# A two-layer S5/RWKV-7 decoder step on one core: transfers and first steps in another order, the token shift spread over scan steps, the feed-forward norm's root applied behind the products

## The chip, the cores and the metric

The kernel runs on one core of one Trainium2 chip. The core has TensorE for matmuls (they write PSUM banks), VectorE and ScalarE for elementwise work, POOL (GpSimd), and SP, which here only issues DMA transfers. In the profile they are PE, DVE, ACT, POOL and SP. The metric is the device time of one execution in microseconds; less is better.

## The reference

Each of two layers mixes tokens by two parallel branches out of one projection, and ends in a feed-forward part: dense in layer 0, a top-2-of-8 mixture in layer 1. There are 272 prompt positions and 8 sample tokens, T = 280 in all, and all data are float32.

```
def rmsnorm(x, g):
    y = xf * lax.rsqrt(jnp.mean(xf * xf, axis=-1, keepdims=True) + RMS_EPS)
    return (y * g.astype(jnp.float32)).astype(x.dtype)
def swiglu(h, w1, w3, w2):
    return (jax.nn.silu(h @ w1) * (h @ w3)) @ w2
# each layer
h = rmsnorm(x, W['norm_mix'][l]);  proj = h @ W['w_in'][l]
# branch A: S5 scan over proj[:, :512]; branch B: RWKV-7 over the next 1792 columns p
prev = jnp.concatenate([shift0[:, None], p[:, :-1]], axis=1)
z = p + (prev - p) * mu                     # the token shift
x = x + m @ W['w_out'][l]                   # m: the gated sum of both branches
h2 = rmsnorm(x, W['norm_ffn'][l])
x = x + swiglu(h2, W['ffn_w1'][j], W['ffn_w3'][j], W['ffn_w2'][j])    # layer 0
```

The root of the norm is one number per token. With g folded into x, h2 @ w1 equals the root times ((x*g) @ w1), so it can be applied to the product.

## The kernel before

Activations lie transposed: the 128 partitions are features, the 280 columns are tokens. A matrix of 1024 features is 8 tiles. All large weights come as slots of 1 MB through a ring of 7 slots in SBUF, issued by SP; a slot is refilled when `weights_used` says that it was read. Each engine has its own instruction list, written out by hand, and they meet only at semaphores. There is no scheduler: an instruction waits behind everything written ahead of it on its engine, and a DMA issue on ScalarE's or POOL's list stands in that list like any other instruction.

**Start.** SP issues the six transfers in `FIRST` and seven ring slots. ScalarE squares the tiles of x (`norm`, i = 0), then issues x0 and 14 constants, then takes the root. TensorE sums the squares with a matrix of ones (the ones products). VectorE takes the reciprocal and writes h in eight products, then runs `discretise` (small steps on 128x32), the products on x0, and `rotation_points`, whose sines ScalarE takes ahead of copying the projection's banks out. TensorE has three banks for projection tiles, so tile n waits for the copy of tile n - 3.

**Projection and scan.** 34 tiles of 8 products each. The first four are the S5 input u, the next 14 are RWKV rows (`prow`), 16 are gates. TensorE alternates: input products of two scan steps (`bu_pair`), four projection tiles, output products (`y5_pair`) of the pair before the last. VectorE runs `scan_pair` for j = 0, 2, ..., 14. POOL writes rotation tables (`rotations`) for each step into one of two buffers, and may do so when VectorE has read the table of two steps earlier. Behind pair 8 stands `shifted`, the whole token shift. Behind the scan come the low-rank products (`lora`), for which TensorE waits until VectorE has read the last input products and ScalarE has done its part on z.

**Feed-forward of layer 0.** Each weight slot is split into a high part (ScalarE, `fw_hi`) and a low part (VectorE, `fw_lo`), the activations likewise (`h_hi`, `h_lo`); a product is three matmuls, so a slot is 48. Before it stand the output projection (8 tiles, each added into x by VectorE), the squares, the ones products, root, reciprocal, eight products into h_f, both splits of h and the split of slot 0. In the loop ScalarE takes silu straight out of PSUM and VectorE multiplies it with the second bank. POOL loads layer 1's small weights (`s5_b`, `s5_c`, `lora_up`) as soon as layer 0's mixer is done.

## Time and profile before

| | us |
|---|---|
| median of 3 runs | 2256.25 |
| lowest, highest | 2254.21, 2258.53 |
| the profiled execution | 2257.98 |
| its span | 2255.8 |
| TensorE busy in it | 2056.7 |
| VectorE busy in it | 1573.3 |
| ScalarE busy in it | 1012.1 |
| POOL busy in it | 359.5 |

The span is the time from the first to the last instruction in one profiled execution. The busy share of an engine is an average over stages that are bound by different things. A timeline row tells when a run of equal instructions starts, how long it lasts, how many there are, and, in brackets, how long the engine idled before it and what released it. A matmul of 128x280 in float32 shows as two records, so a projection tile is x16 and four tiles are x64. PEclk is the TensorE clock that was granted, 1.00 being 2.4 GHz and 0.50 being 1.2 GHz. Layer 0's mixer takes 0 to 500, its feed-forward 500 to 722, layer 1's mixer follows, and the experts fill the rest from about 1,229 on.

### The profile page before, as it was taken

The page shows a single profiled execution, that of the slowest core. Times are in us where ns is not written, and L with a number is a line of the kernel's source. Part 1 is how long each engine was busy: PE and PEld are TensorE (multiplying, and loading weights), DVE is VectorE, ACT ScalarE, POOL GpSimd, SP SyncE. Part 2 cuts the span into 40 slices and gives each one's busy share as a digit, 9 for nine tenths or more (in the row PEclk, how much of TensorE's full clock was granted, in tenths as well). Part 3 has the DMA queues.
Part 4 walks back from the last instruction along what each step waited for, and adds up shares of the span by engine and source line. Part 5 has one row for each costly group of instructions (what it writes and reads, how often), then busy time and mean ns, then how long its engine had stood idle before and what let it go on. Part 6 is the DMA issues. An engine that isn't in the chain of part 4 may idle for free.

```text
span 2255.8 us, 29759 instructions
## 1 busy us (share of the span) xinstructions
PE 2056.7 (91%) x11490; PEld 1690.4 (75%) x11490; DVE 1573.3 (70%) x1960; ACT 1012.1 (45%) x1184; POOL 359.5 (16%) x315
## 2 busy tenths in 40 slices
PE   3998789898999997788895999999999999999996
PEld 2775577778999775577774888888888888888884
DVE  3586766325544777766324889898988889898984
ACT  1012323104433111333103777777767677777773
POOL 0553600200000554501201010101010100100000
PEclk7997999598999998999695999999999999999998
DMA  6333000144443333000142999999999999999990
GB/s 241 112 114 112 3 1 1 59 166 180 169 168 131 112 131 113 3 1 1 40 167 81 365 377 355 354 362 359 357 364 357 360 366 353 366 360 352 364 361 36
DMA packets 71627, 466.71 MB, mean 207 GB/s; under 512 B 12453, under 2 KB 13349, under 8 KB 16325
## 3 DMA queue, kind: packets, MB, share of 16 engines
q1 hardware_dynamic: 62352, 449.11, 53.7%
q0 software_dynamic: 3184, 13.24, 1.5%
q10 hardware_dynamic: 5956, 2.50, 0.4%
q8 instruction: 93, 1.52, 0.3%
q14 instruction: 42, 0.34, 0.0%
HBM read 459.74 MB, written 5.08 MB: 206 GB/s over the span
## 4 chain that ended last, share of the span: by engine, by line
PE 79%; DVE 7%; issue 6%; POOL 4%; ACT 2%; ACTq 1%; DMA 0%; SPq 0%; DVEq 0%; POOLq 0%
PE bank L526 77%; PE bank L1105 1%; ACTq L1183 1%; POOL arena L376 1%; DVE arena L1660 1%; PE bank L673 1%; ACT arena L1168 1%; POOL arena L390 1%; DVE arena L1490 0%; POOL arena L397 0%; DVE ring L1791 0%; DVE ring L1815 0%; DVE ring L1803 0%; ACT ring L1168 0%; POOL arena L408 0%
## 5 line engine op out<-in xcount | busy, mean ns | idle before, releaser
L2065 DVE TENSOR_TENSOR w_lo<-ring,w_hi 128x2048 fp32r<-128x2048 f32 x336 | 768.9, 2293 | 109.1 <-ACT w_hi L1168 108.7
L1168 ACT ACTIVATE w_hi<-ring 128x2048 fp32r<-128x2048 f32 x336 | 643.5, 1916 | 183.2 <-PE bank L526 183.2
L526 PE MATMUL bank<-arena,ring 128*128 128x280 f32 (+1 forms) x1920 | 460.6, 408 | 48.1 <-DVE arena L1490 23.0
L526 PEld LDWEIGHTS bank<-arena,ring 128*128 128x128 f32 (+1 forms) x1920 | 354.8, 190 | 143.4 <-issue 39.1
L1168 ACT ACTIVATE arena<-bank 128x256 f32<-128x256 f32 (+4 forms) x300 | 117.7, 396 | 592.2 <-PE bank L526 576.5
L526 PE MATMUL bank<-w_hi,he_hi 128*128 128x512 f32 x896 | 365.4, 408 | 4.9 <-DVE w_lo L2065 4.9
L526 PE MATMUL bank<-w_hi,he_lo 128*128 128x512 f32 x896 | 353.8, 395 | 0.0
L526 PE MATMUL bank<-w_lo,he_hi 128*128 128x512 f32 x896 | 353.4, 394 | 0.0
L526 PEld LDWEIGHTS bank<-w_hi,he_lo 128*128 128x128 f32 x896 | 169.0, 189 | 39.3
L526 PEld LDWEIGHTS bank<-w_hi,he_hi 128*128 128x128 f32 x896 | 169.1, 189 | 37.2 <-issue 5.3
L526 PEld LDWEIGHTS bank<-w_lo,he_hi 128*128 128x128 f32 x896 | 169.8, 190 | 32.4
L526 PE MATMUL bank<-ring 128*128 128x128 f32 (+6 forms) x1504 | 163.0, 269 | 31.9 <-DVE ring L1791 14.8
L526 PEld LDWEIGHTS bank<-ring 128*128 128x128 f32 (+3 forms) x1504 | 147.6, 171 | 49.7 <-DVE ring L1791 18.4
L526 PE MATMUL bank<-w_hi,at_hi 128*128 128x512 f32 x448 | 176.4, 394 | 0.0
L526 PE MATMUL bank<-w_hi,at_lo 128*128 128x512 f32 x448 | 176.4, 394 | 0.0
L526 PE MATMUL bank<-w_lo,at_hi 128*128 128x512 f32 x448 | 176.2, 393 | 0.0
L526 PE MATMUL bank<-arena 64*64 64x64 f32 (+12 forms) x1472 | 140.2, 307 | 34.8 <-DVE arena L1601 25.4
L526 PEld LDWEIGHTS bank<-arena 64*64 64x64 f32 (+6 forms) x1472 | 102.9, 179 | 76.5 <-issue 32.5
L1168 ACT ACTIVATE ring<-bank 128x256 f32<-128x256 f32 (+4 forms) x210 | 63.0, 358 | 169.2 <-PE bank L526 133.5
L496 POOL CAST rows<-arena 128x1 uint32<-128x1 f32 x8 | 13.9, 1732 | 763.9 <-ACT arena L1168 763.9
L1981 DVE TENSOR_TENSOR fw_lo<-ring,fw_hi 128x2048 fp32r<-128x2048 f32 x33 | 75.6, 2293 | 61.1 <-ACT fw_hi L1168 61.1
L526 PE MATMUL bank<-h_hi,fw_hi 128*128 128x280 f32 x352 | 103.6, 294 | 11.4 <-DVE fw_lo L1981 11.4
(261 smaller groups left out, 2634.9 us busy)
## 6 DMA issues: line engine op xcount, KB each, us to landing
ring<-wstream_dram SPq DMA_DIRECT2D x427, 1024.0 KB, 6.8
s<-s_dram POOLq DMA_DIRECT2D x2, 1024.0 KB, 14.7
o_rw_dram<-arena POOLq DMA_DIRECT2D x2, 1024.0 KB, 5.1
x<-x_dram SPq DMA_DIRECT2D x1, 1120.0 KB, 5.0
y_dram<-arena POOLq DMA_DIRECT2D x1, 1120.0 KB, 4.4
arena<-s_b_dram POOLq DMA_DIRECT2D x2, 512.0 KB, 7.5
arena<-s_c_dram POOLq DMA_DIRECT2D x2, 512.0 KB, 9.4
arena<-lora_up_dram POOLq DMA_DIRECT2D x2, 512.0 KB, 11.4
```

Source lines behind the costliest of these rows:

```text
L376: g.tensor_tensor(tc, ca, cb, ALU.mult)
L390: ins = g.tensor_scalar(chi[:, f, :], z[:, 4 + f, :], col(l, "k_k", f), None, ALU.mult)
L496: nc.gpsimd.tensor_copy(rows[:], slot_iw[:, e % 2, 0:1]).then_inc(S["rows_ready"], 1)
L526: return nc.tensor.matmul(out, lhsT, rhs, start=start, stop=stop, **k)
L673: last = nc.tensor.transpose(pools[4 * i][0:nt, j * P:(j + 1) * P], src, ident[:])
L1105: last = nc.tensor.transpose(pools[2][:, (t % 2) * FW + j * P:(t % 2) * FW + (j + 1) * P], act_e[:, t % 2, j * P:(j + 1) * P], ident[:])
L1168: return nc.scalar.activation(out, in_, func, **k)
L1183: ac.dma_start(t[:], a[n]).then_inc(S["consts"], 16)
L1660: ins = v.tensor_scalar(z[:, c, :], z[:, c, :], col(l, "mu", c), None, ALU.mult)
L1981: v.tensor_tensor(fw_lo[n % 2], slot(FFN_AT + n), fw_hi[n % 2].bitcast(F32), ALU.subtract)\
L2065: v.tensor_tensor(w_lo[n % SPLIT], slot(n), w_hi[n % SPLIT].bitcast(F32), ALU.subtract)\
```

## The change

1. **Transfers.** SP issues lam and tv first, under a semaphore of their own, then x, ones, eps and pv, ring slot 0, x0, the 14 constants, and only then ring slots 1 to 6. ScalarE issues none of them any more. POOL issues s0 behind the fourth table in place of before the first. Layer 1's small weights wait for the end of the feed-forward, since h_lo has moved to where they lie.
2. **First steps.** The discretisation up to the angles and layer 0's rotation points stand ahead of the first norm on VectorE, the rest behind it. `one_mu` holds 1 - mu.
3. **Token shift.** ScalarE writes (1 - mu) p into z as it copies a bank. VectorE adds mu times the previous column in one instruction for each tile, in groups of 4, 4, 4 and 2 behind the pairs 2, 4, 6 and 8.
4. **Feed-forward norm.** h_hi and h_lo are made from x times the gains, tile by tile, as the output projection adds into x. Slot 0 is split ahead of that. TensorE runs slot 0, then the ones products, in bank 4. VectorE multiplies both banks by the root's reciprocal as it takes them out of PSUM, into up_s and act_f; silu reads up_s.

```diff
--- before.py
+++ after.py
-        h_hi, h_lo = half("h_hi", 4480, DC, T), half("h_lo", 2048, DC, T)
+        h_hi, h_lo = half("h_hi", 4480, DC, T), half("h_lo", 8640, DC, T)
+        up_s = ar(7840, 2, T)
         act_hi, act_lo = half("act_hi", 10912, CF, T), half("act_lo", 17072, CF, T)
-        fw_hi = [half(f"fw_hi{i}", at, SLOT) for i, at in enumerate((0, 25280))]
-        fw_lo = [half(f"fw_lo{i}", at, SLOT) for i, at in enumerate((23232, 27328))]
+        fw_hi = [half(f"fw_hi{i}", at, SLOT) for i, at in enumerate((25280, 0))]
+        fw_lo = [half(f"fw_lo{i}", at, SLOT) for i, at in enumerate((27328, 23232))]
...
-        FIRST = [(x, "x"), (lam, "lam"), (ones, "ones"), (eps, "eps"), (pv, "pv"), (tv, "tv")]
+        FIRST = [(x, "x"), (ones, "ones"), (eps, "eps"), (pv, "pv")]
...
+            for t, n in ((lam, "lam"), (tv, "tv")):
+                sp.dma_start(t[:], a[n]).then_inc(S["lam_in"], 16)
             for t, n in FIRST:
                 sp.dma_start(t[:], a[n]).then_inc(S["first_in"], 16)
-
-            for s in range(RING):
+            sp.dma_start(ring[:, 0, :], a["wstream"][0]).then_inc(slot_in[0], 16)
+            sp.dma_start(x0[:], a["x0"]).then_inc(S["x0_in"], 16)
+            for t, n in CONSTS[1:]:
+                sp.dma_start(t[:], a[n]).then_inc(S["consts"], 16)
+            for s in range(1, RING):
...
-                    pool.wait_ge(S["x_ready"], 2 * l - 1)
+                    pool.wait_ge(S["x_ready"], 2 * l)
                 pool.wait_ge(S["first_in"], N_FIRST)
                 pool.dma_start(s5_b, a["s5_b"][l]).then_inc(S["small_w"], 16)
                 pool.dma_start(s5_c, a["s5_c"][l]).then_inc(S["small_w"], 16)
                 pool.dma_start(lora_up, a["lora_up"][l]).then_inc(S["small_w"], 16)
-                pool.dma_start(s0[:], a["s0"][l]).then_inc(S["s0_in"], 16)
-
                 for j in range(JT):
                     rotations(l, j)
+                    if j == 3:
+                        pool.dma_start(s0[:], a["s0"][l]).then_inc(S["s0_in"], 16)
...
-                norm(1 + 2 * l)
+                if l:
+                    norm(1 + 2 * l)
...
-                    pe.wait_ge(S["weights_used"], FFN_AT + n + 1)
+                    if n:
+                        pe.wait_ge(S["weights_used"], FFN_AT + n + 1)
                     if n >= 2:
                         pe.wait_ge(S["act_ready"], n - 1)
                     w_h, w_l = (t[n % 2].rearrange("p (c k m) -> p c k m", c=2, k=DC) for t in (fw_hi, fw_lo))
                     for c in range(2):
                         for k in range(DC):
-                            if n == 0 and c == 0 and k % 4 == 0:
-                                pe.wait_ge(S["h_split"], k // 4 + 1)
+                            if n == 0 and c == 0:
+                                pe.wait_ge(S["split_lo"], k + 2)
                             last = split_products(pools[2 * (n % 2) + c][:, 0:T], (w_h[:, c, k, :], w_l[:, c, k, :]),
                                                   (h_hi[:, k, :], h_lo[:, k, :]), k == 0, k == DC - 1)
+                            if n == 0 and c == 0 and k == 0:
+                                last.then_inc(S["weights_used"], 2)
                     last.then_inc(S["up_ps"], 1)
+                    if n == 0:
+                        norm(1)
...
-                if i == 0:
-                    ac.dma_start(x0[:], a["x0"]).then_inc(S["x0_in"], 16)
-                    for t, n in CONSTS[1:]:
-                        ac.dma_start(t[:], a[n]).then_inc(S["consts"], 16)
                 ac.wait_ge(S["norm_ps"], i + 1)
...
-                    ins = fn(prow[:, n - CA, 1:T + 1], src, ACT.Identity)
+                    if n == CA:
+                        ac.wait_ge(S["pad_zero"], l + 1)
+                    c = n - CA
+                    fn(z[:, c, :], src, ACT.Identity, scale=one_mu[:, l, c:c + 1])
+                    ins = fn(prow[:, c, 1:T + 1], src, ACT.Identity)
...
+                ac.wait_ge(S["bo_out"], 1)
+                ac.wait_ge(slot_in[FFN_AT % RING], 16 * (FFN_AT // RING + 1))
+                fn(fw_hi[0], slot(FFN_AT), ACT.Identity).then_inc(S["ffn_hi"], 1)
+                ac.wait_ge(S["rw_out"], 32)
+                c0 = PV["norm_ffn"][0]
+                for c in range(DC):
+                    ac.wait_ge(S["wo_out"], c + 1)
+                    fn(h_hi[:, c, :], x[:, c, :], ACT.Identity, scale=pv[:, 0, c0 + c:c0 + c + 1]).then_inc(S["split_hi"], 1)
                 norm(1)
-                for q in (slice(0, DC // 2), slice(DC // 2, DC)):
-                    ac.wait_ge(S["h_ready"], DC + q.stop)
-                    fn(h_hi[:, q], h_f[:, q], ACT.Identity).then_inc(S["h_hi_out"], 1)
-                for n in range(S_FUP + S_FDOWN + 2):
+                for n in range(1, S_FUP + S_FDOWN + 2):
                     m = n - 2
                     if 0 <= m < CF:
-                        ac.wait_ge(S["up_ps"], m + 1)
-                        fn(silu_s[:, m % 2, :], pools[2 * (m % 2)][:, 0:T], ACT.Silu).then_inc(S["up_silu"], 1)
+                        ac.wait_ge(S["up_scaled"], m + 1)
+                        fn(silu_s[:, m % 2, :], up_s[:, m % 2, :], ACT.Silu).then_inc(S["up_silu"], 1)
...
+            ac.wait_ge(S["lam_in"], 32)
+            fn(small[:, 2, :], lam[:, 2, :], ACT.Exp).then_inc(S["disc_exp"], 1)
...
-            def shifted(l):
-
-                tt = v.tensor_tensor
-                dve.wait_ge(S["proj_out"], CIN * l + CA + CR)
+            def shifted(l, *tiles):
+
+                dve.wait_ge(S["proj_out"], CIN * l + CA + tiles[-1] + 1)
                 dve.wait_ge(S["pad_zero"], l + 1)
+                for c in tiles:
+                    ins = v.scalar_tensor_tensor(out=z[:, c, 0:TP], in0=prow[:, c, 0:TP], scalar=col(l, "mu", c),
+                                                 in1=z[:, c, 0:TP], op0=ALU.mult, op1=ALU.add)
+                if tiles[-1] < CR - 1:
+                    return
                 dve.wait_ge(S["consts"], N_CONST)
-                tt(z[:, :, 0:TP], prow[:, :, 0:TP], prow[:, :, 1:TP + 1], ALU.subtract)
-                step(tt(z[:, :, TP:T], shift0[:, l], prow[:, :, TP + 1:T + 1], ALU.subtract))
-                for c in range(CR):
-                    ins = v.tensor_scalar(z[:, c, :], z[:, c, :], col(l, "mu", c), None, ALU.mult)
-                step(ins)
-                tt(z, z, prow[:, :, 1:T + 1], ALU.add).then_inc(S["z_ready"], 1)
+                c0 = PV["mu"][0]
+                step(v.tensor_tensor(shift0[:, l], shift0[:, l], pv[:, l, c0:c0 + CR].unsqueeze(2).broadcast_to([P, CR, NS]), ALU.mult))
+                v.tensor_tensor(z[:, :, TP:T], z[:, :, TP:T], shift0[:, l], ALU.add).then_inc(S["z_ready"], 1)
...
-                rotation_points(l)
+                if l:
+                    rotation_points(l)
                 scaled_c(l)
                 for j in range(0, JT, 2):
                     scan_pair(l, j)
-                    if j == 8:
-                        shifted(l)
+                    if 2 <= j <= 8:
+                        shifted(l, *range(2 * j - 4, min(2 * j, CR)))
...
+                def scaled_low(c):
+
+                    c0 = PV["norm_ffn"][0]
+                    dve.wait_ge(S["split_hi"], c + 1)
+                    stt(out=h_lo[:, c, :], in0=x[:, c, :], scalar=pv[:, 0, c0 + c:c0 + c + 1], in1=h_hi[:, c, :].bitcast(F32),
+                        op0=ALU.mult, op1=ALU.subtract).then_inc(S["split_lo"], 1)
+
+                if l == 0:
+                    dve.wait_ge(S["ffn_hi"], 1)
+                    tt(fw_lo[0], slot(FFN_AT), fw_hi[0].bitcast(F32), ALU.subtract).then_inc(S["split_lo"], 1)
+                    dve.wait_ge(S["rw_out"], 32)
                 for n in range(DC):
                     dve.wait_ge(S["wo_ps"], DC * l + n + 1)
                     tt(x[:, n, :], x[:, n, :], pools[4 + n % 4][:, 0:T], ALU.add).then_inc(S["wo_out"], 1)
+                    if l == 0 and n:
+                        scaled_low(n - 1)
+                if l == 0:
+                    scaled_low(DC - 1)
...
-                norm(1, pv[:, 0, PV["norm_ffn"][0]:PV["norm_ffn"][0] + DC], h_f)
-                dve.wait_ge(S["h_ready"], 2 * DC)
-                for i, q in enumerate((slice(0, DC // 2), slice(DC // 2, DC))):
-                    dve.wait_ge(S["h_hi_out"], i + 1)
-                    v.tensor_tensor(h_lo[:, q], h_f[:, q], h_hi[:, q].bitcast(F32), ALU.subtract).then_inc(S["h_split"], 1)
+                dve.wait_ge(S["norm_rt"], 2)
+                step(v.reciprocal(rstd[:, 1, :], rstd[:, 0, :]))
                 added = 0
-                for n in range(S_FUP + S_FDOWN + 2):
+                for n in range(1, S_FUP + S_FDOWN + 2):
                     m = n - 2
                     if 0 <= m < CF:
+                        dve.wait_ge(S["up_ps"], m + 1)
+                        v.tensor_tensor(up_s[:, m % 2, :], rstd[:, 1, :], pools[2 * (m % 2)][:, 0:T], ALU.mult)\
+                            .then_inc(S["up_scaled"], 1)
+                        step(v.tensor_tensor(act_f[:, m % 2, :], rstd[:, 1, :], pools[2 * (m % 2) + 1][:, 0:T], ALU.mult))
                         dve.wait_ge(S["up_silu"], m + 1)
-                        v.tensor_tensor(act_f[:, m % 2, :], silu_s[:, m % 2, :], pools[2 * (m % 2) + 1][:, 0:T], ALU.mult)\
+                        v.tensor_tensor(act_f[:, m % 2, :], act_f[:, m % 2, :], silu_s[:, m % 2, :], ALU.mult)\
...
+            dve.wait_ge(S["lam_in"], 32)
+            discretise()
+            rotation_points(0)
             dve.wait_ge(S["first_in"], N_FIRST)
+            c0 = PV["mu"][0]
+            v.tensor_scalar(one_mu[:], pv[:, :, c0:c0 + CR], -1.0, 1.0, ALU.mult, ALU.add)
             norm(0, pv[:, 0, PV["norm_mix"][0]:PV["norm_mix"][0] + DC], h)
-            discretise()
+            discretise_rest()
```

The rows below are the order of instructions on one engine, as written (no times). First SP's list from its first transfer; `ring` are weight slots, `x<-x_dram 128x512` is x0. Before:

```order
L333 DMA x<-x_dram 128x2240
L333 DMA lam<-lam_dram 128x96
L333 DMA ones<-ones_dram 128x128
L333 DMA eps<-eps_dram 128x2
L333 DMA pv<-pv_dram 128x124
L333 DMA tv<-tv_dram 128x33
L336 DMA ring<-wstream_dram 128x2048 x7
```

and now, up to the second constant and from the last:

```order
L335 DMA lam<-lam_dram 128x96
L335 DMA tv<-tv_dram 128x33
L337 DMA x<-x_dram 128x2240
L337 DMA ones<-ones_dram 128x128
L337 DMA eps<-eps_dram 128x2
L337 DMA pv<-pv_dram 128x124
L338 DMA ring<-wstream_dram 128x2048
L339 DMA x<-x_dram 128x512
L341 DMA blk<-blk_dram 128x128
...
L341 DMA router<-router_dram 128x64
L343 DMA ring<-wstream_dram 128x2048 x6
```

One slot still follows the first six transfers directly; x0 and 14 constants have come between it and the other six.

VectorE's list behind scan pair 8 of layer 0, before (L1632 ends a pair, L1600 begins the next):

```order
L1632 COPY s5out<-arena 128x18 x2
L1657 TENSOR_TENSOR arena<-arena 128x14x272
L1658 TENSOR_TENSOR arena<-shift,arena 128x14x8
L1660 TENSOR_SCALAR arena<-arena,pv 128x280 x14
L1662 TENSOR_TENSOR arena<-arena 128x3920
L1600 TENSOR_TENSOR arena<-bank,arena 128x560
```

and behind pair 2 now, where the first group of the shift stands (L1623 is the old L1600):

```order
L1650 TENSOR_TENSOR arena<-arena 128x280
L1655 COPY s5out<-arena 128x18 x2
L1679 SCALAR_TENSOR_TENSOR arena<-arena,pv 128x272 x4
L1623 TENSOR_TENSOR arena<-bank,arena 128x560
L1624 TENSOR_TENSOR arena<-bank,arena 128x560
```

The block of 17 instructions behind pair 8 has become groups that stand ahead of the next pair's first reads.

VectorE's list from the last output tile into the feed-forward, before (fw_lo_55 and fw_lo_56 are the two buffers):

```order
L1771 TENSOR_TENSOR x<-x,bank 128x280 x8
L1488 RECIPROCAL rstd<-rstd 128x280
L1490 SCALAR_TENSOR_TENSOR arena<-x,pv,rstd 128x280 x8
L1964 TENSOR_TENSOR h_lo<-arena,h_hi 128x1120 x2
L1981 TENSOR_TENSOR fw_lo_55<-ring,fw_hi_53 128x2048
L1981 TENSOR_TENSOR fw_lo_56<-ring,fw_hi_54 128x2048
L1970 TENSOR_TENSOR arena<-arena,bank 128x280
L1981 TENSOR_TENSOR fw_lo_55<-ring,fw_hi_53 128x2048
```

and now, from the last output tile on (the split of slot 0, L1803, stands ahead of the first):

```order
L1807 TENSOR_TENSOR x<-x,bank 128x280
L1798 SCALAR_TENSOR_TENSOR h_lo<-x,pv,h_hi 128x280 x2
L2000 RECIPROCAL rstd<-rstd 128x280
L2021 TENSOR_TENSOR fw_lo_56<-ring,fw_hi_54 128x2048
L2006 TENSOR_TENSOR arena<-rstd,bank 128x280
L2008 TENSOR_TENSOR arena<-rstd,bank 128x280
L2010 TENSOR_TENSOR arena<-arena 128x280
L2021 TENSOR_TENSOR fw_lo_55<-ring,fw_hi_53 128x2048
```

The reciprocal now stands ahead of the low half of slot 1, no longer ahead of that of slot 0, and each slot has three steps on the banks where it had one.

## Rows read from the trace of the kernel before

**Rows 1.** The page: chain of waits by engine.
```profile
PE 79%; DVE 7%; issue 6%; POOL 4%; ACT 2%; ACTq 1%; DMA 0%; SPq 0%; DVEq 0%; POOLq 0%
```

**Rows 2.** Timeline, start; columns: start, length, engine, line, operation, idle before.
```profile
3.72 3.40 SPq L336 DMA_DIRECT2D ring<-wstream_dram  x7
6.99 0.44 ACT L1168 ACTIVATE arena<-x 128x280 f32<-128x280 f32 x1 [4.97 <-DMA tv<-tv_dram]
...
7.57 6.14 PE L526 MATMUL bank<-arena,ones 128*128 128x280 f32 x16 [7.57 <-ACT arena L1168]
...
12.24 3.19 ACTq L1183 DMA_DIRECT2D keep<-keep_dram  x1
...
30.98 1.90 DVE L1488 RECIPROCAL rstd<-rstd 128x280 f32<-128x280 f32 x1 [30.98 <-ACT rstd L1168]
...
33.57 14.33 PE L526 MATMUL bank<-arena,ring 128*128 128x280 f32 x48 [19.87 <-DVE arena L1490]
```

**Rows 3.** Busy time of VectorE in five stretches; columns: stretch, length, busy (count).
```profile
36.29:39.59 3.30, 2.79 (x16) 0.56 0.00 0
48.77:54.72 5.95, 5.70 (x11) 0.84 0.04 15
41.41:60.69 19.28, 18.05 (x46) 0.82 0.16 55
155.46:170.58 15.12, 15.05 (x20) 0.94 0.19 69
839.44:854.57 15.13, 15.06 (x19) 1.00 0.20 70
```

**Rows 4.** Timeline of TensorE, projection of layer 0.
```profile
56.15 5.76 PE L526 MATMUL bank<-arena,ring 128*128 128x280 f32 x16 [8.24 <-ACT arena L1168]
62.49 1.21 PE L526 MATMUL bank<-arena 32*128 32x280 f32 x8 [0.58 <-ACT arena L1168]
...
131.71 15.36 PE L526 MATMUL bank<-arena,ring 128*128 128x280 f32 x64
...
173.31 2.24 PE L526 MATMUL bank<-arena 32*128 32x280 f32 x8 [7.46 <-DVE arena L1601]
...
208.57 10.13 PE L526 MATMUL bank<-arena 64*128 64x280 f32 x24 [4.71 <-DVE arena L1601]
```

**Rows 5.** Timelines of VectorE, then of POOL, in the scan steps.
```profile
125.23 0.73 DVE L1601 TENSOR_TENSOR arena<-bank,arena 128x560 f32<-128x560 f32 x1
...
130.69 0.74 DVE L1620 TENSOR_TENSOR arena<-arena 128x560 f32<-128x560 f32 x1 [0.81 <-PE bank L526]
...
114.56 1.08 POOL L376 TENSOR_TENSOR arena<-arena 128x272 f32<-128x272 f32 x1 [13.24 <-DVE arena L1621]
...
196.13 3.19 POOL L376 TENSOR_TENSOR arena<-arena 128x272 f32<-128x272 f32 x1 [6.78 <-DVE arena L1621]
```

**Rows 6.** Timeline, feed-forward norm and its first slot.
```profile
500.37 3.94 PE L526 MATMUL bank<-arena,ones 128*128 128x280 f32 x16
...
504.94 1.90 DVE L1488 RECIPROCAL rstd<-rstd 128x280 f32<-128x280 f32 x1 [3.92 <-ACT rstd L1168]
506.88 3.46 DVE L1490 SCALAR_TENSOR_TENSOR arena<-x,pv,rstd 128x280 f32<-128x280 f32 x8
...
515.69 0.60 PE L526 MATMUL bank<-h_hi,fw_hi 128*128 128x280 f32 x1 [11.38 <-DVE fw_lo L1981]
...
524.30 0.41 ACT L1168 ACTIVATE arena<-bank 128x280 f32<-128x280 f32 x1 [7.89 <-PE bank L526]
```

**Rows 7.** Timelines of VectorE, then of ScalarE, in steady feed-forward slots.
```profile
563.58 2.29 DVE L1981 TENSOR_TENSOR fw_lo<-ring,fw_hi 128x2048 fp32r<-128x2048 f32 x1 [1.35 <-ACT fw_hi L1168]
...
561.34 0.41 ACT L1168 ACTIVATE arena<-bank 128x280 f32<-128x280 f32 x1 [3.65 <-PE bank L526]
...
567.51 0.41 ACT L1168 ACTIVATE arena<-bank 128x280 f32<-128x280 f32 x1 [3.64 <-PE bank L526]
```

**Rows 8.** TensorE in one stretch: busy (count), granted clock, DMA share, GB/s.
```profile
516.00:520.00 4.00, 4.00 (x18) 0.50 0.82 272
```

55 lines of the change are left out of this document (29 added, 26 removed).

## The prediction

> **What bounds the kernel now.** I read the page's chain of waits first: TensorE carries 79% of it [rows 1], and the last 1,030 us are the experts, which the change leaves alone. So only a stretch ahead of them counts in which TensorE stands idle, or runs at its lower clock because it just did. The timeline shows four such places.
>
> 1. The start. The squares of the first norm begin at 6.99 and the ones products end at 13.71, but VectorE's reciprocal comes only at 30.98 [rows 2]. In between ScalarE's queue issues the constants: from 12.24 on an issue takes 3.2 us, where SP's seven slots took 0.5 each, and the root stands behind them. The first projection tile starts at 33.57. Three tiles later TensorE waits 8.24 us more for a bank, because ScalarE has not yet done the sines of the rotation points; these wait for VectorE's discretisation and its rotation points. The first input products (bu) come at 62.49 [rows 4].
> 2. The token shift of layer 0, one block on VectorE from 155.46 to 170.58 [rows 3]. TensorE waits 7.46 us for the scan step behind it, and 4.71 us before the low-rank products at 208.57 [rows 4].
> 3. The feed-forward norm. The last output tile is done at 500.4, ones products follow to 504.31, and the first feed-forward product starts at 515.69, 11.38 us later [rows 6].
> 4. The token shift of layer 1, 15.1 us again [rows 3].
>
> **The start.** Six transfers are still awaited before the first norm and the last is still the sixth issue, so I leave 6.99 and the end of the ones products at 13.71. Behind the feed-forward norm the same hand-over (products end 504.31, reciprocal 504.94) takes 0.63 us [rows 6]; here it gives 14.35. VectorE has the discretisation (3.5 us with its last step) and the rotation points (5.95) ahead of it [rows 3], started when the lam transfer lands, some 2 us ahead of 6.99 by the order of issues: 5.2 + 3.5 + 6.0 = 14.7, then the small one_mu step. I take 14.9. From reciprocal to first tile is 33.57 − 30.98 = 2.6 us [rows 2], so TensorE starts at 17.5. ScalarE after its root has two exponent and sine steps and the sines of the points, some 5 us with table loads, so it frees banks from about 20, when the first tile is not yet done: the 8.24 us wait goes. Four tiles took 14.33 + 5.76 = 20.1 us [rows 2, 4], of which the second figure holds a restart at the lower clock: 5.76 against 15.36/4 = 3.84 for a tile in full run [rows 4], 1.9 us that go as well. So 18.2 us, and 0.6 for the bank copy as before: bu at 36.3 instead of 62.49. What is late next is VectorE: eight products (3.5) end at 20.4, the rest of the discretisation and the scaling of C take 19.28 − 5.95 = 13.3 [rows 3], to 33.7; 2.6 us of cover are left. **Gain 26.2**; bounds 19 (slots or VectorE late, below) and 29 (no restart at the lower clock at all, another 3 us).
>
> The queues that these steps pass: SP now issues one weight slot, x0 and 14 constants ahead of slots 1 to 6. At SP's 0.5 us an issue [rows 2] slot 1 goes out near 12 and lands before 20; it is needed two tiles after 17.5, at about 26. POOL still issues its three loads behind the six first transfers; only s0 moves, behind the fourth table, where POOL idles 6 us for VectorE before the next one [rows 5]. That costs nothing.
> The Trainium skill (DMA: Bandwidth & Descriptors, Issuing engines are not separate DMA queues) says that DMAs from several engines share the same 16 DMA engines, and that spreading issues saves only the issue time, which is usually small. By that rule alone the move of the constants would be worth next to nothing. The issue row of 12.24 differs in this: issuing itself held ScalarE, at 3.2 us a constant, up to the root whose result VectorE takes at 30.98, because the issuing engine had other work behind it.
>
> **The token shift.** Removed per layer: 15.1 us of VectorE. Added: 14 multiply-adds on 128x272 in groups of 4, 4, 4, 2 behind scan steps. The trace has the same form in the norm's products, 3.46 us for eight, 0.44 each [rows 6]; a group costs 1.8 us. ScalarE writes the scaled copy, 14 more of 0.41 us [rows 7], beside a TensorE tile of 3.84: hidden. In the steady scan steps VectorE waits only 0.81 us for TensorE (130.69, rows 5), so a group does not fit in that. But TensorE needs the banks that a step's last reads (125.23 + 0.73 = 125.96, rows 5) set free only for its next bu, 1.2 us ahead of the tiles of 131.71 [rows 4]: VectorE may fall behind by 4.5 us before TensorE stands. It falls behind by 1.8 − 0.8 = 1.0 us at each of two groups, then by 0.7 at the last: 2.7, and wins 0.8 back in each pair behind. So TensorE no longer stops at 165.9, where its wait began, nor restarts at the lower clock (2.24 us for the 1.21 of a bu in full run). From there it needs 1.2 for bu, 15.4 for four tiles and 1.3 for the output products, so VectorE may turn pair 12 back at 183.8, and POOL starts its last tables at 185.2 in place of 196.13 [rows 5]. From that start to the low-rank products were 12.4 us [rows 4, 5], and are 11.3 where POOL's first multiply takes 1.08 in place of 3.19, as VectorE then loses half of it. That gives 196.5 to 197.6, and up to 1.8 more with the lag kept. Against 208.57 I take 197.7, 10.9 earlier. **Gain 21.8 over two layers**, bounds 8 and 24.
>
> A rule that speaks against it: the groups read two SBUF tensors while POOL builds its tables, also in SBUF. Rows 5 show what that can do: one POOL multiply takes 1.08 us in one place and 3.19 in the other, each time beside VectorE steps of that kind. The Trainium skill (SBUF — State Buffer, Who interferes with whom) says that such VectorE and GpSimd instructions exclude each other for a whole instruction, whichever starts first. The 3.19 agrees with it, the 1.08 looks more like taking turns. Either way what POOL loses to a group is at most its 1.8 us, which is the lag already counted; the rival below has it exposed in full.
>
> **The feed-forward norm.** The first slot's split runs beside the attention output, and h_hi, h_lo are made tile by tile beside 3.84 us tiles. So slot 0 starts at 500.5 and at the upper clock. The clock matters: after the 11 us wait TensorE did 18 products in 4 us, at a granted clock of 0.50, which is 1.2 GHz [rows 8]; later a slot of 48 takes 6.17, that is 31 in 4 us. Slot 0 lasts those 6.17 us (561.34 to 567.51, rows 7), to 506.7; the ones products 3.8, to 510.5. Now the root is exposed, and behind it in the written order the second slot's low half: 0.63 to the reciprocal, 1.9 for it, then 2.3 for the split (rows 6, 7): slot 1 starts at 515.4, after 4.9 us idle, and I let it run as slowly as slot 0 did before (515.69 to 524.24, 8.55), to 523.95. Before, slot 1 ended at 524.24 + 6.17 = 530.4. **Gain 6.5**, bounds 4 (a late slot 2) and 8.8 (no restart at the lower clock).
> Per slot VectorE does two more products of 0.45 us and one of them, 0.5 with its hand-over, stands ahead of the silu. Today the low half is ready at 563.58 + 2.29 = 565.87 and TensorE comes for it when it ends the slot before, at about 567.5: 1.6 us of cover [rows 7], 1.1 after. Nothing more to pay in 22 slots.
>
> **Layer 1's small weights** are now issued after the feed-forward, by x_ready. Their first use stands behind a norm (ones products 3.9, reciprocal 1.9, products 3.5) and the rotation points (5.9): about 15 us [rows 3, 6]. The first six transfers, 1.3 MB, had landed 7 us into the span [rows 2], and these three are 1.5 MB beside ring slots that come one at a time. Cost nothing; bound 4 us, for a landing that takes more than twice as long.
>
> **Sum.** 26.2 + 21.8 + 6.5 = 54.5. The profiled execution took 2257.98 us with a span of 2255.8; it gives 2203.5. The median of the runs is 2256.25, 1.7 below it: **2202 us**.
>
> **Rivals.**
> - VectorE and POOL collide fully (10%): each group's 1.8 us shows on both, TensorE waits again for bu and the tables end later. 14 × 0.44 = 6.2 us a layer back: 2202 + 12 = 2214. For it: 0.81 us of slack. Against: 4.5 us before TensorE stands.
> - Transfers late at the start (9%): SP's issues run at the 3.2 us that ScalarE's had once its queue was full [rows 2]. With some five of them so, slot 1 goes out near 26 and lands some 7 us later, at 33, TensorE waits 7 us and restarts slowly: 2211. Against: the constants then had seven slots in front, now one.
> - The clock stays up at the start and in slot 1 (12%): 3 + 2.3 more, 2196.
> - The start does not do what it says (4%): something else, such as the small weights or the points, still holds the scan; half the 26 us stay, 2215.
> - Slower than before (2%): the slot loop of the feed-forward. If the added steps lengthen the hand-over by more than 1.6 us, TensorE idles in each slot, and should the pauses hold it at the lower level, a slot costs 48 × 4/18 = 10.7 us for 6.2: 22 × 4.5 = 99 us more, 2301. The point is 1.6 us; I count 0.5.
> - The forecast (63%), its own range 2197 to 2208.
>
> The range 2192 to 2214 holds the first three rivals at its edges. About 0.2%, 4.5 us, is what a measurement tells from no change. The small rest, several terms failing at once, goes to both lower outcomes: faster 0.95, same 0.02, slower 0.03.
>
> **What would show it.** In the new profile: ones products to 13.7, reciprocal near 15, first tile near 17.5, first bu near 36; no TensorE wait over 1 us inside the projection; the low-rank products about 37 us earlier than 208.57; feed-forward slot 0 right behind the last output tile, then one wait of about 5 us before slot 1 and none after; the span between layer 1's projection start and its low-rank products about 11 us shorter. A wait of TensorE for a slot near 26, or for VectorE in every feed-forward slot, would make it wrong.

## The result, and the profile after

The changed kernel takes 2189.27 us in the median of 4 runs (2185.01 to 2194.59), the kernel before 2257.33 in the runs beside it: ratio 0.9702, 95% interval 0.9677 to 0.9726, 68 us less. Over all groups of runs one execution of the kernel before took 2414 us at a granted clock of 0.81; it is left out. I had predicted 2202 us in a range of 2192 to 2214. The direction was right, the time lies below the range. The profiled execution is the slowest of the four, 2194.59 us with a span of 2192.8, so it stands 63.0 us below the profiled one of before. A second profile of the same kernel, taken in the experiments, has a span of 2185.1: 70.7 us below.

The page's chain of waits, now 85% TensorE (79% in [rows 1]), and no share left on ScalarE's queue (ACTq, 1% before):

```profile
PE 85%; issue 5%; DVE 4%; POOL 3%; ACT 1%; DMA 0%; SPq 0%; DVEq 0%; POOLq 0%; ACTq 0%
```

The start, in the timelines of ScalarE, VectorE, TensorE and SP's queue (columns as in [rows 2]):

```profile
3.05 0.23 ACT L1181 ACTIVATE arena<-lam 128x32 f32<-128x32 f32 x1 [1.03 <-DMA tv<-tv_dram]
8.11 2.72 ACT L1181 ACTIVATE arena<-x 128x280 f32<-128x280 f32 x8 [4.83 <-DMA pv<-pv_dram]
...
11.88 0.70 DVE L1585 TENSOR_TENSOR arena<-arena 128x528 f32<-128x528 f32 x1
...
15.40 1.90 DVE L1506 RECIPROCAL rstd<-rstd 128x280 f32<-128x280 f32 x1 [2.73 <-ACT rstd L1181]
17.34 4.27 DVE L1508 SCALAR_TENSOR_TENSOR arena<-x,pv,rstd 128x280 f32<-128x280 f32 x8
...
8.69 6.15 PE L533 MATMUL bank<-arena,ones 128*128 128x280 f32 x16 [8.69 <-ACT arena L1181]
18.00 15.73 PE L533 MATMUL bank<-arena,ring 128*128 128x280 f32 x64 [3.16 <-DVE arena L1508]
34.31 1.21 PE L533 MATMUL bank<-arena 32*128 32x280 f32 x8 [0.58 <-ACT arena L1181]
...
12.33 2.84 SPq L343 DMA_DIRECT2D ring<-wstream_dram  x6
```

The reciprocal comes at 15.40 instead of 30.98 [rows 2] and the first input products (bu) at 34.31 instead of 62.49 [rows 4]. Both waits of before are gone, the one for the root and the 8.24 us for a bank. VectorE's rotation points end at 12.58, before the root is there, so VectorE waits 2.73 us for the root. The squares begin only at 8.11, where I had left them at 6.99, and the ones products end at 14.84 instead of 13.71; why the last of the first transfers lands later, no run shows. The slots go out from 12.33 on at under 0.5 us each, and TensorE waits for none.

The token shift of layer 0, groups of multiply-adds on VectorE, POOL's table steps, and TensorE up to the low-rank products:

```profile
109.72 2.90 DVE L1679 SCALAR_TENSOR_TENSOR arena<-arena,pv 128x272 f32<-128x272 f32 x4
...
127.28 1.31 DVE L1679 SCALAR_TENSOR_TENSOR arena<-arena,pv 128x272 f32<-128x272 f32 x2
...
110.68 0.84 POOL L384 TENSOR_TENSOR arena<-arena 128x272 f32<-128x272 f32 x1
...
145.65 0.65 POOL L384 TENSOR_TENSOR arena<-arena 128x272 f32<-128x272 f32 x1
...
156.79 1.08 POOL L383 TENSOR_TENSOR arena<-arena 128x272 f32<-128x272 f32 x1 [7.72 <-DVE arena L1644]
...
156.34 7.81 PE L533 MATMUL bank<-arena,ring 128*128 128x280 f32 x32
168.32 8.86 PE L533 MATMUL bank<-arena 64*128 64x280 f32 x24 [2.99 <-DVE arena L1624]
```

TensorE no longer stops inside the projection, and the wait ahead of the low-rank products is 2.99 us instead of 4.71 [rows 4]. A group of four takes 2.90 us, not the 1.8 I had worked out from 0.44 each [rows 6]: beside it a step of POOL takes 0.84 instead of the 0.65 it takes alone. So both are slowed. The Trainium skill (SBUF — State Buffer, Who interferes with whom) says that of such a pair the one that comes later is blocked for the whole of the other's instruction. If the two alternated by that rule, four multiply-adds would take 4 × (0.44 + 0.65) = 4.4 us by my estimate; the row shows 2.90.

The groups cost TensorE nothing all the same. VectorE had more room than the 0.81 us that I read: in each pair it also waited for POOL's table. A steady pair before, and the pair behind a group now:

```profile
142.15 0.74 DVE L1600 TENSOR_TENSOR arena<-bank,arena 128x560 f32<-128x560 f32 x1 [2.45 <-POOL arena L382]
```

```profile
114.80 0.74 DVE L1623 TENSOR_TENSOR arena<-bank,arena 128x560 f32<-128x560 f32 x1 [0.45 <-POOL arena L389]
```

With the 0.81 us for TensorE that is some 3.2 us a pair before the change, against a group of 2.9.

The feed-forward norm and one steady slot, TensorE and VectorE:

```profile
453.77 0.50 PE L533 MATMUL bank<-h_hi,fw_hi 128*128 128x280 f32 x1
460.17 3.94 PE L533 MATMUL bank<-arena,ones 128*128 128x280 f32 x16
468.95 0.60 PE L533 MATMUL bank<-h_hi,fw_hi 128*128 128x280 f32 x1 [4.85 <-DVE fw_lo L2021]
...
464.67 1.90 DVE L2000 RECIPROCAL rstd<-rstd 128x280 f32<-128x280 f32 x1 [8.94 <-ACT rstd L1181]
466.61 2.29 DVE L2021 TENSOR_TENSOR fw_lo<-ring,fw_hi 128x2048 fp32r<-128x2048 f32 x1
...
486.54 2.29 DVE L2021 TENSOR_TENSOR fw_lo<-ring,fw_hi 128x2048 fp32r<-128x2048 f32 x1 [1.28 <-ACT fw_hi L1181]
...
489.95 0.45 DVE L2006 TENSOR_TENSOR arena<-rstd,bank 128x280 f32<-128x280 f32 x1 [0.77 <-PE bank L533]
```

Slot 0 (453.77) follows the last output tile at once, one wait of 4.85 us stands before slot 1 where 11.38 stood before slot 0 [rows 6], and none after it. The steady low half ends at 486.54 + 2.29 = 488.83. The slot before ends at about 489.9, where VectorE gets its banks (489.95), so the cover is 1.1 us.

**What was not edited changed as well.** Below is the same cut through the whole program in windows: length of the stretch, busy time of PE, PEld, VectorE, ScalarE and POOL (counts), granted clock, DMA share, GB/s. First the kernel before: low-rank products to the first transposes of layer 0; transposes to the last output tile; layer 1's transposes to the routing's reciprocal.

```profile
208.57:271.29 62.72, 50.89 (x200) 37.07 (x200) 47.18 (x79) 23.21 (x38) 24.68 (x16) 0.83 0.01 3
271.29:500.37 229.08, 203.16 (x1704) 166.62 (x1705) 109.56 (x267) 48.47 (x143) 35.57 (x15) 0.86 0.13 47
951.54:1184.27 232.73, 207.70 (x1720) 170.44 (x1720) 104.83 (x269) 49.39 (x145) 35.66 (x15) 0.86 0.14 51
```

The changed kernel, the same three stretches:

```profile
168.32:225.77 57.45, 45.72 (x201) 34.15 (x201) 46.68 (x79) 23.27 (x38) 24.38 (x16) 0.90 0.02 8
225.77:453.77 228.00, 203.53 (x1704) 167.48 (x1705) 109.04 (x274) 51.02 (x144) 35.63 (x15) 0.86 0.13 48
887.72:1122.73 235.01, 210.16 (x1720) 172.06 (x1720) 104.72 (x269) 49.39 (x145) 35.63 (x15) 0.85 0.14 50
```

And the changed kernel in its second profile, the latter two:

```profile
227.88:452.24 224.36, 199.73 (x1704) 164.14 (x1705) 106.28 (x274) 50.74 (x144) 35.85 (x15) 0.88 0.13 48
886.68:1115.79 229.11, 203.86 (x1720) 167.13 (x1720) 101.98 (x269) 49.11 (x145) 35.81 (x15) 0.88 0.14 52
```

The counts of products are the same but for one record, the lengths are not, and the granted clock goes with them: layer 1's mixer tail takes 235.0 us at 0.85 and 229.1 at 0.88 in two executions of one program. Length times (1 − clock) gives the time given up at the lower clock: 35.3 and 27.5 us. The difference is 7.8 us (the second decimal of the clock leaves it open by some 2), that in length 5.9.

Length less busy time is 24.9 us in the one execution and 25.3 in the other. So TensorE did not wait longer, its products took longer. Some 2.5 us of the 5.9 come from one place. In the changed kernel's first profile:

```profile
1006.30:1013.10 6.80, 6.64 (x86) 4.21 (x84) 3.45 (x11) 1.79 (x3) 2.13 (x1) 1.00 0.01 2
1013.10:1019.90 6.80, 6.76 (x77) 5.04 (x76) 5.16 (x5) 2.24 (x4) 6.42 (x3) 0.50 0.01 2
```

and in the second profile, from about the same product on as the lower row:

```profile
1009.40:1016.20 6.80, 6.76 (x111) 5.58 (x110) 3.65 (x11) 2.12 (x4) 6.42 (x3) 1.00 0.01 2
```

TensorE was busy 6.64 of the 6.80 us ahead of the fall, at last on products of form 64x32. The lower clock came without a pause, and in one execution of two.

With marks at the same instructions the profiled differences come apart so (us saved against before; left the first, right the second profile of the changed kernel):

```
                                             predicted   1st    2nd
start, to the first bu                          26.2     28.2   27.3
projections with the token shift, 2 layers      21.8     24.5   24.5
feed-forward, last output tile to reciprocal     6.5      6.3    6.0
edited places together                          54.5     58.9   57.8
low-rank products to transposes, layer 0         0        5.3    4.0
transposes to last output tile, layer 0          0        1.1    4.7
layer 1: reciprocal to first bu                  0       -1.4   -1.6
layer 1: low-rank products to routing            0       -2.4    3.5
experts and rest                                 0        1.5    2.2
span                                            54.5     63.0   70.7
```

### The profile page after: what moved, and what is told of

The parts are those of the page before. It is cut to its first block, busy times and chain, and to the rows that moved or that the text cites. A ratio compares the mean times of both kernels' runs of the same rounds, so it can differ in the third digit from the quotient of the medians.

```text
span 2192.8 us, 29865 instructions
## 1 busy us (share of the span) xinstructions
PE 2044.8 (93%) x11490; PEld 1684.1 (77%) x11490; DVE 1588.6 (72%) x2001; ACT 1024.9 (47%) x1218; POOL 351.7 (16%) x315
## 4 chain that ended last, share of the span: by engine, by line
PE 85%; issue 5%; DVE 4%; POOL 3%; ACT 1%; DMA 0%; SPq 0%; DVEq 0%; POOLq 0%; ACTq 0%
PE bank L533 83%; PE bank L1118 1%; PE bank L680 1%; POOL arena L397 1%; POOL arena L404 0%; DVE ring L1831 0%; DVE ring L1855 0%; ACT ring L1181 0%; POOL arena L415 0%; DVE ring L1843 0%; ACT arena L1181 0%; DVE arena L1508 0%; PE bank L1068 0%; PE bank L825 0%; POOL arena L408 0%
## 5 line engine op out<-in xcount | busy, mean ns | idle before, releaser
L533 PE MATMUL bank<-arena,ring 128*128 128x280 f32 (+1 forms) x1920 | 453.7, 404 | 23.1 <-DVE arena L1508 6.3
L533 PEld LDWEIGHTS bank<-arena,ring 128*128 128x128 f32 (+1 forms) x1920 | 350.3, 187 | 115.3 <-issue 21.5
L1181 ACT ACTIVATE arena<-bank 128x256 f32<-128x256 f32 (+4 forms) x278 | 108.6, 394 | 382.6 <-PE bank L533 367.4
```

What stands on the lines that cost most here:

```text
L533: return nc.tensor.matmul(out, lhsT, rhs, start=start, stop=stop, **k)
L1181: return nc.scalar.activation(out, in_, func, **k)
```

## The experiments

16 kernels were run. Stretches of their profiles in us, named by where they end; the projection of each layer runs from its first bu to its low-rank products, "low-rank" from these to the transposes, "FF" from the end of the last output tile (first ones product or first feed-forward product) to layer 1's reciprocal, "start 1" from there to layer 1's first bu, "tail 1" from layer 1's transposes to the routing's reciprocal, "experts" from there to the reciprocal of the last norm, some 13 us before the end:

```
kernel          start  proj.0 low-rank0 tail 0    FF   start1 proj.1 low-rank1 tail 1 experts
before           62.5  146.1   62.7     229.1   226.1   20.0  146.4   58.6    232.7  1058.6
changed          34.3  134.0   57.5     228.0   219.9   21.4  134.0   58.7    235.0  1057.2
changed_again    35.2  134.0   58.7     224.4   220.2   21.6  134.0   58.7    229.1  1056.4
start_only       35.4  146.1   62.7     229.1   226.1   20.0  146.1   58.7    229.1  1056.5
shift_only       62.7  134.0   58.8     224.5   226.3   20.1  136.2   58.7    232.2  1056.5
ffn_only         62.3  146.1   62.7     228.9   220.0   21.5  146.1   63.2    236.8  1058.8
consts_only      45.9  146.0   62.7     229.1   226.1   20.0  146.4   58.6    232.8  1058.8
steps_only       52.9  146.1   62.2     229.0   226.1   20.0  146.1   58.7    229.1  1056.5
shift_block      33.9  139.8   58.4     227.1   220.2   19.9  139.9   58.4    231.9  1056.6
ffn_pad          34.4  134.0   57.3     224.4   242.7   20.2  134.0   58.5    232.1  1056.5
fill_mixer       35.6  134.0   55.2     224.2   220.2   21.6  134.0   58.0    233.6  1058.9
fill_ffn         34.4  134.0   57.4     230.3   217.7   18.5  134.0   58.5    232.9  1058.6
pad_start        36.3  134.0   57.5     226.9   220.2   19.9  134.0   57.4    231.9  1056.6
pad_layer1       35.1  134.0   58.7     224.3   220.2   23.3  134.0   57.4    231.9  1056.7
early_fill       37.6  134.0   58.0     228.9   213.6   18.5  134.0   56.8    233.8  1058.8
early_low        34.1  134.0   57.5     226.9   213.6   21.5  134.0   58.7    229.0  1056.5
early_norms      34.1  134.0   57.4     226.9   213.6   18.5  134.0   58.6    232.8  1058.6
early_norms_lora 34.5  134.0   56.9     228.9   213.6   18.5  134.0   56.8    233.7  1058.9
```

Times are medians; the kernel before took 2255.6 to 2255.9 us in each group of runs.

**The changed kernel again.** No edit.

> The changed kernel once more, as the control beside the parts. Its profiled execution was 63 us shorter than the kernel before's, the medians 68. If the last 5 us are chance of the executions (TensorE's granted clock was 0.945 in the profiled one, 0.948 to 0.949 in the others), this profile shows a time of 2185 to 2191 with a clock near 0.949, and the difference sits in some stretches behind waits; if the profile itself costs the time, it is 2194 again at 0.945.

2192.45 us (2185.57 to 2202.01), ratio 0.9726 (0.9706 to 0.9746). The profiled execution took 2186.92 at a clock of 0.948, and another one 2202.01 at 0.941, so it is the execution and not the profile. Over nine runs the changed kernel goes from 2185 to 2202 with a median of 2190.4, where the kernel before keeps within 2253 to 2259.

**The parts alone.** Each is the kernel before with one part of the change's diff.

> The kernel before with the start's part alone (orders of transfers, discretisation and rotation points first). Theory: the gain is what the trace of the changed kernel shows at the first bu, 28 us, and every stretch behind it is as before: 2229 (2227 to 2231). Rival: TensorE's clock comes back sooner further on as well, up to the 6 us that the changed kernel won in layer 0 outside the edited places: 2223.

> The kernel before with the token shift's part alone. Theory: 12.1 us in layer 0 and 12.4 in layer 1 up to the low-rank products, and some 3 us more in layer 0 behind them, because TensorE waits 3 us there instead of 4.7 and comes back to its upper clock sooner: 2257 - 28 = 2229. Rival: the 3 us belong to the start or are chance, and only 24.5 come: 2232.5. What I predicted was 21.8: 2235.

> The kernel before with the feed-forward's part alone (root applied behind the up products, first slot split early, layer 1's small weights issued after the feed-forward). Theory: 6.5 us up to layer 1's norm, given back by 1.4 in layer 1's first tiles: 2251. Rival: the small weights, issued later, cost layer 1 some 3 us: then layer 1 from its reciprocal to its first bu is longer than the 20.0 us of before, and the total is 2254.

start_only 2224.19 (ratio 0.9853, 0.9839 to 0.9867), shift_only 2225.98 (0.9866, 0.9852 to 0.9880), ffn_only 2256.08 (0.9985, 0.9962 to 1.0009; 12 runs, nine from 2252.54 to 2261.37 at a clock of 0.930 to 0.934 and three from 2238.76 to 2239.51 at 0.939). The edited stretches give in each what they give in the changed kernel: 27.1, 12.1 and 10.2, and 6.2 us. The totals do not: 31.7, 29.9 and nothing. In start_only layer 1's tail and the experts are 3.7 and 2.2 us shorter, in shift_only layer 0's low-rank stretch and tail 4.0 and 4.6. In ffn_only layer 1 gives back 1.5 + 4.5 + 4.1 us in stretches whose code is that of before. Its row for layer 1's tail shows the clock at 0.85:

```profile
950.60:1187.37 236.77, 209.74 (x1720) 171.44 (x1720) 110.00 (x268) 49.39 (x145) 35.57 (x15) 0.85 0.13 50
```

My theory (the stretches alone) falls in all three; of the rivals only that of start_only (2223) came near. The rival of ffn_only (late small weights) falls too: its low-rank stretch and tail lost more than its start, and in the changed kernel the last of the three loads is issued at 671.2 and takes 7.0 us to land (median of its two issues), while the first bu starts at 695.0.

**The start in two halves.** consts_only takes the constants off ScalarE, steps_only moves discretisation and points (and the transfers of lam and tv, which these need). In short, in words in place of the longer lines:

```
-                if i == 0:                       # consts_only, ScalarE
-                    ac.dma_start(x0[:], ...)     # and the 14 others
+            sp: slot 0, x0, 14 constants, slots 1 to 6
+            sp: lam, tv first                    # steps_only
+            discretise(); rotation_points(0)     # steps_only, VectorE, ahead of norm(0)
```

> The kernel before with the constants' issues alone moved from ScalarE to SP, behind weight slot 0; discretisation and rotation points stay behind the norm. Theory: the reciprocal comes at 14.4 to 15, the first tile near 17.5, and VectorE, which now has discretisation, points and scaling of C (22.8 us) between the norm's products and the first scan step, holds the scan: the first bu at 36 to 37 but the second up to 7 us later, so that 20 to 24 of the 28 us come: 2232 to 2236. Rival: ScalarE's issues were all of it, 28 us and 2226 (the start's part alone gave 2224). Second rival: a constant's issue takes 3.2 us on SP too and slot 1 comes late: above 2236.

> The kernel before with the first steps alone moved: lam and tv first, VectorE's discretisation and rotation points ahead of the norm; the constants are still issued by ScalarE between squares and root. The start's part as a whole gave 27 us to the first bu, the constants alone 16.6. Theory: the root stays held to about 31 us, so the reciprocal comes at 31 and the first tile at 33.6 as before; only the 8.24 us wait for a bank goes (and with it the restart), first bu at 52 to 54, total 2246 to 2248. Rival: with the constants' issues next to the tables' loads the reciprocal moves too, bu below 50.

consts_only 2240.55 (0.9924, 0.9911 to 0.9938): it gains less than the 20 to 24 us that I gave it. TensorE:

```profile
17.05 11.56 PE L529 MATMUL bank<-arena,ring 128*128 128x280 f32 x48 [3.23 <-DVE arena L1489]
39.63 5.70 PE L529 MATMUL bank<-arena,ring 128*128 128x280 f32 x16 [11.02 <-ACT arena L1171]
45.91 1.21 PE L529 MATMUL bank<-arena 32*128 32x280 f32 x8 [0.58 <-ACT arena L1171]
```

The first tile comes at 17.05, and then the wait for a bank behind the sines grows from 8.24 [rows 4] to 11.02 us: I had looked for the cost at the scan, and it stands at ScalarE's queue, as in the kernel before. steps_only 2237.88 (0.9915, 0.9900 to 0.9930), first bu at 52.9 as expected, the total 9 us below what I expected, of which layer 1's tail and the experts hold 5.8. ScalarE's issues and TensorE:

```profile
12.99 3.97 ACTq L1185 DMA_DIRECT2D keep<-keep_dram  x1
...
34.79 17.52 PE L528 MATMUL bank<-arena,ring 128*128 128x280 f32 x64 [20.68 <-DVE arena L1492]
```

So 16.6 us to the first bu are the constants' and 9.6 the first steps'; together 27 to 28.

**The shift in one block.** `if j == 8: shifted(l, *range(CR))` in place of the four groups.

> The changed kernel with all 14 multiply-adds of the token shift in one block behind the fifth pair of scan steps, where the old block stood. Theory (spreading matters because VectorE may fall behind by 4.5 us only): the block takes 6 us alone, up to 11 beside POOL's tables, TensorE stops once for 1 to 6 us and the stretch from the first bu to the low-rank products is 136 to 140 us instead of 134.0: 4 to 10 us more in all, 2194 to 2200. Rival: the gain came from the fewer operations alone, 134 to 135 and 2190.

2201.43 (0.9780, 0.9759 to 0.9800), 11 us above the changed kernel. VectorE and TensorE:

```profile
126.83 8.50 DVE L1679 SCALAR_TENSOR_TENSOR arena<-arena,pv 128x272 f32<-128x272 f32 x14
...
138.47 1.21 PE L533 MATMUL bank<-arena 32*128 32x280 f32 x8 [1.25 <-DVE arena L1624]
173.69 1.73 PE L533 MATMUL bank<-arena 64*128 64x280 f32 x3 [7.48 <-DVE arena L1624]
```

An 8.5 us block makes TensorE stand for 1.25 us, and the lag that VectorE keeps shows once more ahead of the low-rank products, 7.48 instead of 2.99 (the row shows the first 3 of its 24 records). Of the 12.1 us a layer, the fewer operations alone give 6.2 and the spreading 5.8.

**The feed-forward's cover.** Four more `step(v.tensor_tensor(act_f..., rstd..., bank))` ahead of the scaled product.

> The changed kernel with four more VectorE products of 0.5 us each ahead of the scaled product in every feed-forward slot: 2.1 us into a hand-over whose cover I put at 1.1 us. Theory: TensorE waits 1.0 us in each of some 20 slots, stays at its upper clock, 20 us more: 2210. Rival (the slower case of the prediction): the short pauses hold the clock down, a slot of 48 products takes 10.7 us instead of 6.2, over 90 us more: 2285. Second rival: VectorE's 22 low halves and x adds in the down slots absorb it, under 5 us.

2213.76 (0.9816, 0.9801 to 0.9831), 23 us above. TensorE waits in each slot, as in this row of its timeline:

```profile
488.53 0.40 PE L533 MATMUL bank<-h_hi,fw_hi 128*128 128x280 f32 x1 [0.79 <-DVE fw_lo L2023]
```

The window over two such slots has the granted clock at 1.00:

```profile
486.00:498.00 12.00, 10.42 (x79) 9.96 (x78) 10.04 (x16) 3.04 (x5) 0.00 (x0) 1.00 0.34 107
```

A slot takes 7.24 instead of 6.17 us: 2.1 added, 1.0 to be seen, so the cover was 1.1. Pauses of 0.79 us, one in each 7.24, did not bring the lower clock here. Of the slower rival the point holds (0.5 counted and 1.1 left are its 1.6 us), its price of 99 us does not.

**Pauses filled.** Products that nobody reads in waits of TensorE:

```
+            fill(0, 5)      # ahead of lora(l)            fill_mixer
+            fill(0, 3)      # ahead of glu(l)             fill_mixer
+            fill(6, 9)      # behind norm(1), ffn slot 0  fill_ffn
+            fill(2, 6)      # behind norm(2)              fill_ffn
```

> The changed kernel with products that nobody reads (ones by a constant, 0.48 us each) put where TensorE waits 2.99 us ahead of the low-rank products (5 of them) and 1.95 us ahead of the GLU (3), both layers. Theory: the pause is what brings the lower clock, so the low-rank products take 5.8 us instead of 8.9 to 10.1 and the stretch from them to the first pair's transposes 54 to 55 us instead of 57.5 to 58.7; 3.5 a layer, 2183 where the changed kernel gives 2190. Rival: the narrow products themselves (64 rows) bring it, the pause does not: the stretch stays at 57.5 to 58.7, or gets longer where fillers run late; 2190 or more.

> The changed kernel with such products in the 4.85 us wait ahead of feed-forward slot 1 (9 of them) and in the 3.2 us wait ahead of layer 1's first tile (6). Theory (lower clock after a pause): slot 1 takes 6.2 us instead of 8.6, and layer 1's first four tiles 15.4 instead of 18.2 to 18.8: 5 us together, 2185. Rival (what a restart takes at one place is chance of the execution): these two stretches shrink but others grow as much, 2190 and a spread as wide as the changed kernel's 2185 to 2202.

fill_mixer: low-rank products in layer 0 without the lower clock, 5.53 us for 8.86:

```profile
169.60 5.53 PE L533 MATMUL bank<-arena 64*128 64x280 f32 x24 [0.45 <-DVE arena L1631]
```

The stretch falls to 55.2 in layer 0, but in layer 1 only from 58.7 to 58.0, and the total is 2194.99 (0.9727, 0.9713 to 0.9740): no gain. So at this place the pause brings the lower clock and not the narrow products: with the wait filled they run at 1.00, where they ran at 0.61 in the changed kernel. What is saved there can come back at the next wait. fill_ffn: 2185.97 (0.9690, 0.9672 to 0.9709). The feed-forward takes 217.7 for 219.9 and layer 1's start 18.5 for 21.4, at full clock:

```profile
673.76:692.27 18.51, 17.60 (x74) 13.60 (x73) 17.45 (x27) 3.75 (x6) 6.01 (x10) 1.00 0.27 102
```

That is 5.1 us as expected, and the total is 4.4 below the changed kernel's 2190.4, though the intervals of the ratios overlap.

**A mere shift of the work.** 5 unread products (2.4 us) ahead of the first bu, of layer 0 or of layer 1.

> The changed kernel with 5 products that nobody reads (0.48 us each, 2.4 us together) between the fourth projection tile and the first input products of layer 0. Nothing behind that point is edited. Sum of terms: 2.4 us more, 2192 to 2193, and every stretch behind the first bu as long as in one of the executions of the changed kernel. Theory (what a restart of TensorE's clock costs hangs on when it falls, so a shift of all the work re-deals it): the stretches with restarts (low-rank products to transposes, pair stage and tail, layer 1's first tiles) change by 1 to 8 us each although their code is the same, and the total may be anything from 2183 to 2200; the projection stretch stays at 134.0.

> The changed kernel with 5 unread products (2.4 us) ahead of layer 1's first input products. Everything up to layer 1's first tiles runs as in the changed kernel. Theory (a shift re-deals what the restarts behind it cost): the stretch from layer 1's transposes to the routing's reciprocal takes another of its values (229.1 to 236.8 us so far for one code, with the granted clock at 0.88 to 0.85), while the projection's stays 134.0. Rival (the value belongs to how the two layers' mixers follow each other, not to such a shift): it stays within 229 to 235 as in the two executions of the changed kernel and the total is 2.4 us more, 2192.

pad_start 2192.55 (0.9716, 0.9702 to 0.9729), pad_layer1 2191.44 (0.9716, 0.9703 to 0.9730): in the total nothing stands out. In the profiles stretches behind the pad have other lengths than in either profile of the changed kernel: layer 1's start 19.9 for 21.4 and 21.6, its low-rank stretch 57.4 for 58.7, its tail

```profile
886.99:1118.92 231.93, 206.72 (x1720) 169.81 (x1720) 101.92 (x269) 49.23 (x145) 35.72 (x15) 0.87 0.14 51
```

with pad_layer1, which up to layer 1's start runs as changed_again does, stretch for stretch. That fits the theory, but one profile each can't part a shift's effect from chance: the tail has two lengths without any edit. The lengths are no even scatter either. In the table layer 1's tail takes 229.0 to 229.1 us in four kernels, 231.9 in three and 232.7 to 232.9 in four, though their code in it is the same up to line numbers.

**Versions meant to be faster.** early_low splits the second feed-forward slot ahead of the root:

```
+                if i == 1:                                   # ScalarE, between squares and root
...
+                    fn(fw_hi[1], slot(FFN_AT + 1), ACT.Identity).then_inc(S["ffn_hi"], 1)
...
+                dve.wait_ge(S["ffn_hi"], 2)                  # VectorE, ahead of the reciprocal
...
+                v.tensor_tensor(fw_lo[1], slot(FFN_AT + 1), fw_hi[1].bitcast(F32), ALU.subtract).then_inc(S["weights_used"], 1)
```

and ScalarE's high half of slot 2 ahead of the first silu. early_fill adds fills ahead of low-rank products, GLU, transposes and layer 1's first tile; early_norms has early_low and fills behind both norms; early_norms_lora also 5 products ahead of the low-rank ones.

> A version meant to beat the changed kernel. Second feed-forward slot split ahead of the root (ScalarE's high half behind the squares, VectorE's low half ahead of the reciprocal, third slot's high half behind the root), so TensorE goes from slot 0 and the ones products straight into slot 1; and unread products in four waits of TensorE: ahead of the low-rank products (5), the GLU (3), the first transposes (12) and layer 1's first tile (6). Theory: the 4.85 us wait and the restart of 2.3 us go, less up to 1.4 us ahead of slot 2: feed-forward from its first product to layer 1's reciprocal 214 us instead of 220; layer 1's start 18.5 instead of 21.4; low-rank to transposes 55; the pair stage behind the filled wait 1 to 2 us less a layer: 13 us in all, 2177. Rival: the pair stage and the tail re-deal their 6 us, 2183.

> The changed kernel with the second feed-forward slot split ahead of the root and nothing else. Theory: the pause of 4.85 us and its restart go, 6.4 us less from the feed-forward's first product to layer 1's reciprocal (213.6 instead of 220.0), 2184 where the changed kernel gives 2190. Rival: the 6.4 us are lost again in layer 1's restarts, 2188 or more.

> The version before with 6 unread products behind the ones products of the first norm and of layer 1's norm, in the 3.2 us in which TensorE waits for the first tile. Theory: both first tiles start at the upper clock in every execution, the first bu at 33.9 to 34.4 (33.9 to 37.6 so far), layer 1's reciprocal to its first bu in 18.5 us (19.9 to 21.6 so far), 2.5 us less in the mean: 2181.5. Rival: the fill of the first norm runs late (products there are slowed to 0.87 us) and holds the first tile back: first bu at 35 or more, 2184.

> The same with 5 unread products ahead of the low-rank products as well (none ahead of the GLU or the transposes). Theory: these took 5.5 us for 8.9 where filled, so the stretch from them to the transposes is 54 to 55.5 us instead of 57.5 to 58.7 in both layers: 2176. Rival: the clock falls in the waits behind them all the same (the filled stretch of layer 1 was 58.0 before), 2180.

early_fill 2187.97 (0.9694, 0.9681 to 0.9707), early_low 2180.71 (0.9680, 0.9660 to 0.9701), early_norms 2183.26 (0.9680, 0.9666 to 0.9693), early_norms_lora 2178.52 (0.9654, 0.9634 to 0.9673), the fastest, 12 us below the changed kernel; only its interval lies wholly below both of the changed kernel's. In all four the feed-forward takes 213.6 us, 6.3 less, at full clock (early_low):

```profile
452.44:666.01 213.57, 212.27 (x1618) 210.18 (x1616) 115.09 (x133) 85.23 (x98) 1.63 (x3) 1.00 0.48 171
```

Layer 1's start keeps its expected 18.5 too where it is filled. The low-rank stretch does not: 56.8 to 56.9 in early_norms_lora, where I expected 54 to 55.5, with a total between theory and rival. early_low came 3 us lower than expected. Missed are early_fill's total, 11 us above what I expected (its profiled start was slow, 37.6, and the fills ahead of GLU and transposes brought nothing), and early_norms, no faster than early_low although 3.0 us shorter in layer 1's start: its profile has 3.8 us more in layer 1's tail and 2.1 in the experts.

## Why the prediction was wrong

**Right: the places and their mechanisms.** The root freed from ScalarE's issues, the bank wait gone with the sines, no wait for a slot, TensorE never standing in the projection, slot 0 behind the last output tile and one wait before slot 1, 1.1 us of cover in the slots, small weights at no cost (layer 1's start is 18.5 us when filled, less than the 20.0 of before). The root, the bank wait, the spreading and the cover were shown to be causes, by consts_only, steps_only, shift_block and ffn_pad; the others are read from the rows.

**Right by luck: the reciprocal near 15.** I had VectorE's own work hold it (14.7, and 14.35 for the root). VectorE was done at 12.7, the ones products ended 1.1 us later than I had left them, and the root held the reciprocal. The two errors partly cancelled, and 15.40 came out.

**Terms mis-sized, 3 to 4 us.** Start: I gave four tiles 18.2 us, with a slow beginning, from 17.5. They began at 18.00 and took 15.73 at a granted clock of 1.00, so most of what the rival "the clock stays up" gave the start came: 2.0 us more gain (1.1 in the second profile, where they took 17.02 at 0.90). The 2.6 us of cover that I left VectorE there were not there: it turned to the first bu at 37.26, 1.7 us after TensorE had ended them, which cost TensorE nothing. Shift: 24.5 us, not 21.8, just outside its bounds of 8 to 24. I kept part of VectorE's lag up to the low-rank products (197.7, where my own working allowed 196.5). A group took 2.9 us and not 1.8, but VectorE's waits for POOL's tables (2.45 us a pair), which I had not counted as room, took it up; by the last pair there was no lag, and POOL's first multiply took 1.08 us, the case in which my working gives 196.5. Feed-forward: 6.0 to 6.3 for 6.5.

**The step that failed: "Sum. 26.2 + 21.8 + 6.5".** It subtracts the edited stretches and takes all others as before. They were not: together 4.1 us shorter in one profile and 12.9 in the other, and with parts alone 9 us longer (ffn_only), 6 shorter (start_only) and 11 shorter (shift_only). These stretches hold many short waits and many narrow products, and in them TensorE goes down to 1.2 GHz and back; clock time given up is 27.5 to 35.5 us in layer 1's tail alone. The filled wait shows that a pause brings the lower clock at the low-rank products. The two profiles of one program show that it also comes while TensorE is busy, and that the price of the same code differs by 5.9 us with nearly the same idle time, 24.9 and 25.3 us. I had the mechanism as a rival (the clock stays up, 2196), but only in two places inside the edits, and gave no width to the 580 us of low-rank stretches and mixer tails. The edited terms could not have reached the result: their three upper bounds, 29, 24 and 8.8, make 61.8 us, 2194 to 2195, and the median is 2189.27. The profiled execution, 2194.59, lies inside the range, so it took both, 3 to 4 us of mis-sized terms and the rest outside the edits, to bring the median 2.7 us below it.

The Trainium skill (TensorE: Matmul & The Clock Gate, What's actually happening) says that the cost of a cold start varies from run to run and that for modelling the penalty is under 1% of a typical span. The first half agrees with the executions here. The second does not: at a mean granted clock of 0.933 the kernel before gives up 0.067 × 2255.8 = 151 us, 6.7% of its span, and the changed one 0.055 × 2192.8 = 121. These are upper bounds, since TensorE also idles at the lower clock. Between the two tails 7.8 us given up went with 5.9 us of time; at that rate the estimate is still 5% for the kernel before.

**Left open.** Why the medians of the changed kernel and of its parts fall mostly to the short side of these stretches. That the shift of the work in time decides it, rather than chance of the execution, was not shown. Nor is it known what made the clock fall at some places in one execution and not in the other.

## What to carry to other kernels

Price the pauses of TensorE twice, as idle time and as lower clock behind them, and give every stretch with many short waits or narrow products its own width even when its code isn't touched; a part worth 6 us can measure as nothing, as ffn_only did. Judge such parts by the length of their own stretch between two marks, and not by the total: the projection with the spread shift took 134.0 us in every profile and layer but one (136.2), and the changed feed-forward, where nothing more was done to it, 219.9 to 220.2. When a queue's work is moved away, ask at once what else stands in front of the same engine: the constants alone gave 16.6 of 27 us, because the sines then waited longer.

## What the runs showed of the hardware

TensorE can be busy and still at its lower clock. In layer 0's tail of the changed kernel, 376 to 396, it is busy 18.38 of 20 us at 0.50:

```profile
376.00:396.00 20.00, 18.38 (x219) 17.97 (x219) 2.81 (x7) 1.08 (x3) 6.83 (x6) 0.50 0.01 2
```

In groups by form, what it does there is products of 16 to 64 rows:

```profile
L533 PE MATMUL bank<-ring 16*64 16x64 f32 x48 | 7.0, 315 | 0.0
L533 PE MATMUL bank<-ring 16*64 16x16 f32 x48 | 6.2, 258 | 0.9 <-DVE ring L1967 0.9
L533 PE MATMUL bank<-arena 64*64 64x1 f32 x80 | 4.4, 242 | 0.0
```

ScalarE's issues of x0 and the constants take 0.36 to 0.60 us each for the first ten and 2.3 to 4.0 for the last five in steps_only, where seven slots stand on SP's queue as in [rows 2]; SP issues the fourteen constants in 0.35 to 0.68 us each when one slot is ahead.
